# A normalisation step moved nine matmuls earlier in two projection stages, and the SBUF working area laid out from another starting byte

## The reference, cut to what matters

```
# first layer
x = x + g_a * (jnp.concatenate([attn_x, hyo_x], axis=-1) @ p["w_out"])
x = x + g_f * conv_ffn(modulate(rmsnorm(x, p["norm_ffn"]), sh_f, sc_f), p)
# second layer
x = x + mixed @ w_out[l]
x = x + conv_glu(rms_norm(x, norm2_g[l]), w_ffn_up[l], ...)

def rms_norm(x, gain):
    xf = x.astype(jnp.float32)
    y = xf * lax.rsqrt(jnp.mean(xf * xf, axis=-1, keepdims=True) + EPS)
    return (y * gain.astype(jnp.float32)).astype(x.dtype)
```

## Time and profile before

| what | value |
|---|---|
| median of 3 runs | 3468.92 us (3468.44 to 3470.12) |
| the profiled execution's own time | 3470.12 us |
| its span, first to last instruction | 3468.2 us |
| PE busy | 3225.0 us, 93% of the span |
| DVE busy | 2253.4 us, 65% |
| ACT busy | 1277.1 us, 37% |
| POOL busy | 942.5 us, 27% |
| mean granted TensorE clock | 0.962 |
| data moved by DMA | 391.66 MB, mean 113 GB/s |

### The profile page before, as it was taken

The page is one execution under the profiler, slowest core; times in us unless marked ns, Lnnn a source line. Parts: engine busy times, 40 slices in busy tenths (PEclk is TensorE's granted clock), DMA queues, the critical chain, the costliest instruction groups (busy, mean ns, idle before and its releaser), DMA issues.

```text
span 3468.2 us, 37507 instructions
## 1 busy us (share of the span) xinstructions
PE 3225.0 (93%) x14700; PEld 2527.2 (73%) x14700; DVE 2253.4 (65%) x2729; ACT 1277.1 (37%) x1937; POOL 942.5 (27%) x890
## 2 busy tenths in 40 slices
PE   6978998898988999999999999999889989999999
PEld 3657777566766778888887788865447777888887
DVE  5455444786775697776345866677763599989533
ACT  3322111554222343333234432357551344444322
POOL 1310210022442134332010244421653214333101
PEclk9879999899998999999999999999899999999999
DMA  4433244010432522224443334551003422222543
GB/s 145 146 128 134 94 168 163 19 43 37 140 122 86 182 98 81 84 85 149 146 155 110 118 114 131 191 184 49 29 23 137 149 88 91 85 79 79 196 133 127
DMA packets 110952, 391.66 MB, mean 113 GB/s; under 512 B 14423, under 2 KB 17047, under 8 KB 110392
## 3 DMA queue, kind: packets, MB, share of 16 engines
q1 hardware_dynamic: 62120, 218.77, 19.4%
q0 software_dynamic: 48656, 170.49, 14.1%
HBM read 306.30 MB, written 82.90 MB: 112 GB/s over the span
## 4 chain that ended last, share of the span: by engine, by line
PE 60%; DVE 10%; issue 2%; ACT 2%; POOL 2%; DMA 0%; ACTq 0%; POOLq 0%; DVEq 0%
PE PS L369 18%; PE PS L371 18%; PE PS L370 18%; PE PS L3051 2%; DVE HL L326 2%; PE PS L3012 1%; PE PS L3034 1%; POOL Sc L3260 1%; DVE E L3186 1%; DVE QR L1407 1%; ACT HL L310 0%; PE PS L2674 0%; DVE HT L1803 0%; DVE kt L1425 0%; DVE kt L1427 0%
## 5 line engine op out<-in xcount | busy, mean ns | idle before, releaser
L369 PE MATMUL PS<-H,HL 128*128 128x512 f32 x1920 | 764.5, 398 | 50.9 <-DVE H L580 12.3
L326 DVE TENSOR_TENSOR HL<-RAW,HL 128x1024 fp32r<-128x1024 f32 (+1 forms) x442 | 501.6, 1136 | 405.4 <-ACT HL L310 400.0
L370 PE MATMUL PS<-H,HL 128*128 128x512 f32 x1920 | 755.2, 393 | 0.0
L371 PE MATMUL PS<-H,HL 128*128 128x512 f32 x1920 | 754.4, 393 | 0.0
L310 ACT ACTIVATE HL<-RAW 128x1024 fp32r<-128x1024 f32 (+1 forms) x442 | 374.5, 848 | 1008.8 <-PE PS L371 915.2
L369 PEld LDWEIGHTS PS<-H,HL 128*128 128x128 f32 x1920 | 365.0, 190 | 142.8 <-issue 35.1
L371 PEld LDWEIGHTS PS<-H,HL 128*128 128x128 f32 x1920 | 365.4, 190 | 77.6
L370 PEld LDWEIGHTS PS<-H,HL 128*128 128x128 f32 x1920 | 365.7, 190 | 76.4 <-issue 2.0
L369 PE MATMUL PS<-HT,HL 128*128 128x512 f32 x720 | 282.7, 393 | 17.9 <-DVE rows L2125 15.8
L370 PE MATMUL PS<-HT,HL 128*128 128x512 f32 x720 | 281.6, 391 | 0.0
L371 PE MATMUL PS<-HT,HL 128*128 128x512 f32 x720 | 281.3, 391 | 0.0
(11 more groups left out here) (382 smaller groups left out, 5405.3 us busy)
## 6 DMA issues: line engine op xcount, KB each, us to landing
RAW<-in_w_up SPq DMA_DIRECT2D x100, 512.0 KB, 3.6
RAW<-in_w_down SPq DMA_DIRECT2D x88, 512.0 KB, 3.6
RAW<-in_w_proj SPq DMA_DIRECT2D x48, 512.0 KB, 3.7
scr_hid<-hidr POOLq DMA_DIRECT2D x36, 512.0 KB, 3.0
HTf<-scr_hid POOLq DMA_DIRECT2D x72, 256.0 KB, 3.7
RAW<-in_w_wmodr SPq DMA_DIRECT2D x32, 512.0 KB, 4.5
RAW<-in_w_wout SPq DMA_DIRECT2D x26, 512.0 KB, 3.7
scr_res<-HTf POOLq DMA_DIRECT2D x48, 256.0 KB, 3.2
```

The costliest lines, as they stand in the source:

```text
L326: e.tensor_tensor(lo, part_source(k, j, x)[0], hi.bitcast(F32), ALU.subtract).then_inc(*k.low.mark(j, x))
L369: e.matmul(out, lh, rh, start=first, stop=False)
L370: e.matmul(out, lh, rl, start=False, stop=False)
L371: return e.matmul(out, ll, rh, start=False, stop=last)
```

## The change

There are two edits. In `pe_halves`, turn 12, the split of the turn's eight input blocks around the spread is moved from 7 and 1 to 4 and 4. In `build`, `rest` is rounded up to a multiple of 512 bytes counted from byte 0 of the partition, where it was a multiple of 512 bytes counted from `base`.

```
@@ pe_halves
         if t == 12:
-            part(t, u, 0, 7)
+            part(t, u, 0, 4)
             free = half_spread(k, e, O, free, 0)
-        x = part(t, u, 4 if t < 2 * O.begun else 7 if t == 12 else 0, 8)
+        x = part(t, u, 4 if t < 2 * O.begun or t == 12 else 0, 8)
@@ build
-        rest = base - (base - place[0]) // 512 * 512
+        rest = -(-place[0] // 512) * 512
```

## The result

The changed kernel took 3494.38 us, median of 4 runs (3490.72 to 3500.78), against 3469.52 for the kernel before (3468.44 to 3471.56, 4 runs). The ratio is 1.0073 with a 95% interval of 1.0054 to 1.0092: 19 to 32 us slower. The forecast was 3473.1, between 3464 and 3482. The profiled execution took 3498.6 us, its span was 3496.7, so 28.5 us more span than in the profile before.

What follows compares the result with a forecast made beforehand. PE was taken as the bound, busy for 93% of the span. Stops of 2.46, clock 1.68 and layout 0 made 4.14 us, giving 3474.3 for the profiled execution and 3473.1 us for the median, range 3464 to 3482.

Steps and rivals of the forecast that it cites:

- The stop: At the spread of turn 12, PE waits 1.23 us for DVE's reciprocal in each layer, 2.46 us together.
- the earlier spread: Turn 12's spread starts 0.81 us earlier, but nobody waits for its result, so a gain is excluded.
- the slack: In turn 12 before the change, 0.86 us between the reciprocal's end and the spread's start.
- The clock: Behind a new stop PE's granted clock may fall to 0.79 for 8 us; one of two taken, 1.68 us.
- the 4.14: Forecast total in us for the whole kernel: 2.46 for stops, 1.68 for the clock, 0 for the working area.
- The working area: Moving it 128 bytes lower was taken as 0 us, with -12.8 and +12.8 as the ends.
- the DVE rows: DVE operations of 128x1024: 1213 ns mixing both positions, 1217 ns with all operands at 128; read as showing no position effect.
- The count of 4272: Feed-forward matmuls reading their moving operand from the working area: 720 x 3 from `HT` and 704 x 3 from `hsr`.
- the ends: Bounds on the working-area term, -12.8 and +12.8 us, from 3 ns on each of 4272 feed-forward matmuls.
- The case: Rival: new positions slow the feed-forward matmuls in `up` and `down`, 12.8 us at 3 ns each, total 3485.8; chance 0.15.
- The DMA rule: Descriptors off a 256-byte multiple pay an extra partial transaction; two DMA pieces on the chain would save 0.2 us.

Runs made afterwards that it cites:

- e10_six: The kernel before with turn 12 cut 6 and 2 around the spread instead of 7 and 1; ratio 1.0000 (0.9991 to 1.0009).
- e11_factor: e1_split with DVE's scaling and reciprocal put ahead of the weight split of turn 12; against the kernel before, ratio 1.0002 (0.9993 to 1.0011).
- e1_split: The kernel before with the first edit alone, turn 12 cut 4 and 4, working area in its old place; 3472.69 us against 3468.72, ratio 1.0013.
- e2_layout: The kernel before with the second edit alone, working area at a multiple of 512 bytes, turn 12 cut 7 and 1; 3493.28 us, ratio 1.0078.
- e4_map: A program of matmuls alone, not the kernel's computation, with 32 pairs of weight and moving-operand positions; 226.7 to 233.3 ns per matmul.
- e5_fine: The matmul-only program with weights at 0 and 80 bytes, moving operand in steps of 16 and 4 bytes; 226.7 ns at the lowest with weights at 0.

## Why the prediction was wrong, point by point

**The stop: right.** 1.23 us per layer were worked out; the trace has 1.16 of idle time in each, counted from the end of the 0.39 us of the last matmul instead of 0.32 us behind its start, which is the same stop. Nothing absorbed it up to the next spread (27.01 and 28.24 us), and the earlier spread paid nothing back. Its input came when the rows of before said, and e10_six and e11_factor bear out the slack.

**The clock: right in size, not in place.** 1.68 us for one slow stretch more, which is what the profile has, but behind an old stop and not behind a new one. Where they fall differs from profile to profile, and e1_split with +1.4 to +7.6 us holds the 4.14.

**The working area: wrong, and this is the step that failed.** The prediction gave it 0, "since the DVE rows are the nearest that differ in position at all, and they show nothing". They were rows of another engine. They did tell the truth about DVE, whose L580 has the same 1213 ns after, and nothing about PE. In the trace before, all three-part matmuls (lines 369 to 371) had the moving operand and the weights at the same position modulo 512, so no row had the new relation. A quantity that never varied in the trace can't be read from it as harmless. The count of 4272 left out the 384 matmuls on `QR`, too; they added 2 us on PE and nothing to their stage. The term measured +23 to +31 us (e2_layout), where the ends were 12.8 either way. They were too narrow because they were 3 ns between the groups' mean durations, two groups whose positions agreed alike; the real difference in distance is 5.7 to 6.1 ns. The case was among the rivals, with the right mechanism in words, the weights' place against the moving operand's, and a chance of 0.15; its price of 16.9 us in all, 3485.8, was short by 9.

**The DMA rule.** In the earlier trace rows the two pieces took 3.78 and 3.59 us. In the changed kernel, with `kt` at a multiple of 256 bytes, the chain has

```profile
974.43 3.64 DMA kt<-scr_hy
...
1090.56 3.63 DMA kt<-scr_hy
```

The sum is 7.27 against 7.37 us. The Trainium skill, "DMA: Bandwidth & Descriptors", section "How a descriptor splits into AXI transactions", is where the prediction's estimate of 0.2 us less comes from. The trace can't decide it: in the chains of the kernel's variants the same two pieces sum to 7.08 to 7.27 us in the four with `kt` at a multiple of 256, and to 6.97 to 7.78 in the six with it at 128 beyond.

## What to carry to other kernels

Keep the start of the moving operand and of the weights equal modulo 256 bytes in streams of matmuls like these (fp32r, 128x128 weights, 512 moving columns, weights at multiples of 128 bytes); 128 bytes of padding were worth 0.8% here. Other types were not measured, and with 256 columns it did not pay. In a trace, read the distance between starts in a stream without gaps, not the waits or the busy share, which was 93% before and after. And when an edit moves addresses, ask which engine's operands change their places against each other, and measure it alone if no row has the new relation.

## What the runs showed of the hardware that was not expected

Matmuls of 128x128 weights and 128x512 moving elements (written as fp32r) ran 226.7 to 227.1 ns apart when both operands' starts agreed modulo 256 bytes, and 229.1 to 233.3 ns apart in steps of 64 bytes when they didn't (e4_map), at a granted clock of 1.00, with no other engine at work and a DMA share of 0.00. In the fine map 226.7 came again at a distance of 240 bytes, and off the multiples of 16 up to 239.6 with the weights at 0 and 240.0 with them at 80 (e5_fine). Behind a restart, streams that agree start a little longer apart too: in the kernel before, behind the sums of turn 12 (1169.97, 1170.20, 1170.44 us) and behind the spreads, the first six to nine distances at full clock were mostly 0.23 to 0.24 us before they fell to 0.227. The same few long distances come when a stream out of step ends and one in step begins: after the change 14% of the distances on `H` were above 228 ns, against 5% before, though neither `H` nor its weights had moved, and the added ones are the first three in the blocks behind `HT`. With a moving operand of 256 columns the order is reversed, 120.0 ns where the starts agree and 118.6 at 128 bytes.
